# Expert weights loaded with consecutive rows to a partition, and transposes that pick every eighth or second column

## The reference, cut to what matters

```python
def routed_experts(hf, idx, wts, w_gate, w_up, w_down):
    # assignments (token, expert) sorted by expert, padded to blocks of 128 of one expert each
    def one_block(args):
        tok_b, gate_b, e = args
        xb = xpad[tok_b]                                        # (128, 1024)
        hb = jax.nn.silu(xb @ w_gate[e]) * (xb @ w_up[e])       # (1024, 256) each
        return (hb @ w_down[e]) * gate_b[:, None]               # (256, 1024)
    out = lax.map(one_block, ...)
    return jax.ops.segment_sum(out, tok, num_segments=T + 1)[:T]
```

## Time and profile before

| | |
|---|---|
| median of three runs | 3056.81 us |
| the profiled execution's own time | 3048.61 us |
| its span, first to last instruction | 3046.6 us |
| mean granted TensorE clock | 0.926 |
| TensorE busy | 2628.0 us (86%) |
| VectorE busy | 1775.5 us (58%) |
| ScalarE busy | 1059.2 us (35%) |
| GpSimd busy | 937.6 us (31%) |
| moved by the transfers | 519.10 MB, mean 170 GB/s |

### The profile page before, as it was taken

How to read it: one execution, slowest core, us unless ns; L and a number is a source line. 1 busy time by engine, 2 the same in 40 slices (tenths; PEclk the granted TensorE clock), 3 DMA queues, 4 the chain that set the end, 5 groups by cost and what they waited for, 6 DMA issues and landing times.

```text
span 3046.6 us, 55986 instructions
## 1 busy us (share of the span) xinstructions
PE 2628.0 (86%) x11778; PEld 2009.8 (66%) x11779; DVE 1775.5 (58%) x3601; ACT 1059.2 (35%) x2213; POOL 937.6 (31%) x1175
## 2 busy tenths in 40 slices
PE   6898898878887739999999999999998999999930
PEld 1175675566567328877788777877887878878820
DVE  1025886787778653265554566666645554455457
ACT  1022222221211123254444455555544443444411
POOL 0022213423340442323333233333233233333347
PEclk9999898989896759999999999999999999999965
DMA  7961001101101225578886798898977877768665
GB/s 261 333 241 46 31 35 56 42 35 42 42 8 70 87 85 149 110 216 226 236 231 189 213 275 258 250 278 257 275 193 220 248 213 199 193 194 231 153 201 195
DMA packets 255945, 519.10 MB, mean 170 GB/s; under 512 B 18238, under 2 KB 154391, under 8 KB 255732
## 3 DMA queue, kind: packets, MB, share of 16 engines
q1 hardware_dynamic: 199108, 327.34, 31.3%
q0 software_dynamic: 56768, 191.00, 26.3%
HBM read 387.00 MB, written 131.99 MB: 170 GB/s over the span
## 4 chain that ended last, share of the span: by engine, by line
PE 60%; issue 11%; DVE 10%; POOL 8%; ACT 4%; DMA 3%; ACTq 2%; DVEq 1%; SPq 0%; POOLq 0%
PE zb L1483 28%; PE mx L1483 14%; DVE mx L918 4%; PE zb L1317 4%; PE tp L1496 4%; POOL list_d L515 4%; PE mx L1339 3%; PE zb L1281 2%; ACT b_wh L803 2%; DMA b_big<-in_w_ada 2%; PE zb L1432 1%; DVE b_wl L1183 1%; PE ly L1529 1%; POOL b_pa L488 1%; POOL b_fst L477 1%
## 5 line engine op out<-in xcount | busy, mean ns | idle before, releaser
L1483 PE MATMUL zb<-b_wh,b_xh 128*128 (+1 forms) x1456 | 588.6, 404 | 32.7 <-DVE b_wl L1183 29.2
L601 POOL DMA_INDIRECT acc_d<-b_ob,b_sidx x180 | 301.3, 1674 | 998.1 <-DVE b_ob L1208 518.3
L1483 PE MATMUL zb<-b_wh,b_xl 128*128 (+1 forms) x1456 | 575.1, 395 | 0.0
L1483 PE MATMUL zb<-b_wl,b_xh 128*128 (+1 forms) x1456 | 574.1, 394 | 0.0
L1183 DVE TENSOR_TENSOR b_wl<-b_win,b_wh (+1 forms) x780 | 481.0, 685 | 154.7 <-ACT b_wh L803 154.7
L803 ACT CAST b_wh<-b_win (+1 forms) x780 | 419.7, 621 | 150.7 <-issue 86.8
L918 DVE SCALAR_TENSOR_TENSOR mx<-b_a_buf,b_wdw,mx 128x256 f32<-128x256 f32 x928 | 364.2, 481 | 0.0
L1317 PE MATMUL zb<-b_hT,b_win 128*128 128x256 f32 x1536 | 342.9, 386 | 0.8 <-DVE b_mrow L878 0.8
L1483 PEld LDWEIGHTS zb<-b_wh,b_xh 128*128 128x128 f32 x1456 | 277.3, 190 | 88.1 <-issue 35.4
L1160 DVE SCALAR_TENSOR_TENSOR b_hh<-b_sgx,b_lt,zb 128x256 f32<-128x256 f32 x181 | 86.6, 479 | 418.5 <-ACT b_sgx L788 417.5
L1317 PEld LDWEIGHTS zb<-b_hT,b_win 128*128 128x128 f32 x1536 | 296.9, 194 | 46.1 <-ACT b_mixP L666 1.7
(11 more groups left out here) (245 smaller groups left out, 3160.6 us busy)
## 6 DMA issues: line engine op xcount, KB each, us to landing
b_win<-in_w_gate SPq DMA_DIRECT2D x64, 1024.0 KB
b_win<-in_w_up SPq DMA_DIRECT2D x64, 1024.0 KB
b_win<-in_w_down SPq DMA_DIRECT2D x64, 1024.0 KB
b_big<-in_w_ada SPq DMA_DIRECT2D x12, 2048.0 KB, 8.9
acc_d<-b_x1b SPq DMA_DIRECT2D x1, 9216.0 KB, 35.8
b_xin<-in_x_prompt SPq DMA_DIRECT2D x16, 512.0 KB, 3.3
b_big<-in_w_ada_final SPq DMA_DIRECT2D x4, 2048.0 KB, 8.0
b_xres<-in_x_prompt SPq DMA_DIRECT2D x16, 512.0 KB
```

Source lines behind the costliest of these rows:

```text
L601: G.indirect_dma_start(acc_d, bass.IndirectOffsetOnAxis(ap=sidx[i][:, 0:1], axis=0), ob[i][:], None, compute_op=ALU.add).then_inc(S["scatb ...
L1483: last = M.matmul(o, lhs, rhs, start=(first and n == 0), stop=(final and n == len(terms) - 1))
```

## The change

The three weight loads read consecutive rows for a partition: partition p of group k now gets input row 8 p + k of gate and up, and row 2 p + k of down. A partition's rows of one matrix are then 8 KB that lie together in DRAM. On the chip nothing moves: group k still stands in unit k, and each 1 KB row of gate lies beside one of up. To match, the k-th token transpose takes columns k, k + 8, k + 16 and so on, and the k-th hidden transpose columns k, k + 2 and so on. Counts of instructions and transfers, queues and waits stay. The shared expert's weights go through the same function.

```diff
         def load_w(set_, gate, up, down):
-            sp.dma_start(stage_gu[:, set_, 0:UG, 0, :], gate.rearrange("(k p) n -> p k n", p=P)).then_inc(S["w_landed"], 16)
-            sp.dma_start(stage_gu[:, set_, 0:UG, 1, :], up.rearrange("(k p) n -> p k n", p=P)).then_inc(S["w_landed"], 16)
-            sp.dma_start(stage_d[:, set_].rearrange("p (k n) -> p k n", k=KE), down.rearrange("(k p) n -> p k n", p=P)).then_inc(S["w_landed"], 16)
+            sp.dma_start(stage_gu[:, set_, 0:UG, 0, :], gate.rearrange("(p k) n -> p k n", p=P)).then_inc(S["w_landed"], 16)
+            sp.dma_start(stage_gu[:, set_, 0:UG, 1, :], up.rearrange("(p k) n -> p k n", p=P)).then_inc(S["w_landed"], 16)
+            sp.dma_start(stage_d[:, set_].rearrange("p (k n) -> p k n", k=KE), down.rearrange("(p k) n -> p k n", p=P)).then_inc(S["w_landed"], 16)
...
-                    last = M.transpose(tp[h][:, kk * P:(kk + 1) * P], xg[j][:, k * P:(k + 1) * P], ident[:])
+                    last = M.transpose(tp[h][:, kk * P:(kk + 1) * P], xg[j][:].rearrange("t (p k) -> t k p", k=KD)[:, k, :], ident[:])
...
-                last = M.transpose(ly[:, k * P:(k + 1) * P], hh[:, k * P:(k + 1) * P], ident[:])
+                last = M.transpose(ly[:, k * P:(k + 1) * P], hh[:].rearrange("t (p k) -> t k p", k=KE)[:, k, :], ident[:])
```

## The result

The changed kernel takes 3059.14 us (median of 20 runs, 3054.20 to 3066.40); the kernel before takes 3054.85 us beside it (20 runs, 3047.42 to 3060.17). The ratio is 1.0016, with a 95% interval of 1.0009 to 1.0023: some 5 us longer, between 2.7 and 7.0. The ratio lies inside the 0.2% (6 us) that the prediction called no change; the upper end of the interval is just outside it. The prediction said 3168 us, 109 us too much. What happened is its rival (1), the load that stays hidden, whose time was 3057 with 3051 to 3063 around it. That the time lies in the stated range of 3050 to 3215 is owed to the room made for this rival, not to the sum.

The account below looks back on a forecast made before the run. TensorE was taken to bound the expert stage. Slower token-transpose loads added 144 us, stalls gave back 33, transfers and hidden transposes counted nothing: +111 us on 3056.8, so 3168 us, range 3050 to 3215.

Parts of the forecast that it names:

- rival (1): Token transposes: a gap at most doubles the weight load, which stays hidden under the identity pass; 3057 us, chance 0.31.
- the sum: Whole kernel: net +111 us, giving 3160 us for the profiled execution and 3168 us on the median's scale.
- What bounds the kernel: Expert stage: TensorE sets the pace, busy 1723.65 of 1790 us; added TensorE time reaches the end unless a stall swallows it.
- The transfers are worth nothing: Weight loads: they wait for buffers, not buffers for loads, so faster loads gain nothing; bound -22.1 us.
- Rival (3): Weight loads matter after all and the load path hides the gap: up to 22 us faster, around 3040 us; chance 0.06.
- Rival (4): Larger reads push the scatters back until output buffers fill: about 3150 us with a hidden load; chance 0.04.
- The identity pass of 110 ns: Token transposes: streaming the identity, not loading the weights, sets their pace, so each load has 110 ns to hide in.
- the two rows: Transpose load records, 30 columns in 96 ns and 128 in 140: streaming 0.45 ns a column, 57 ns for 128.
- The price of a gap: Token transposes' weight load: 1.74 ns for each separate place, from VectorE's 256-byte-step reduction; 223 ns for 128 columns.
- the term of 144 us: Token transposes: seven loads a block each pay 113 ns, 0.79 us a block, over 182 blocks.
- The hidden transposes take nothing: Two hidden transposes a block: 8 bytes is nearer to the contiguous 4 than to 256, so no cost; upper bound 20 us.
- The cover by stalls: TensorE's idle time ahead of down's first load, 38.9 us in 54 turns, gives back an estimated 33 us.

Follow-up runs that it names:

- the probe: Kernel before plus chains of transposes, matmuls and VectorE additions at several column steps; weight load 62 ns side by side, 110 at step 8, 147 at step 64.
- the kernel whose stalls ahead of down are gone: Kernel before with ScalarE's and VectorE's table reads moved earlier, 3017.89 us; with the change on top 3030.94 us, ratio 0.9927 to the kernel before.

## Why the prediction was wrong

**What bounds the kernel: right.** The stage goes at TensorE's pace: 0.05 us more a block shows at the end as 8.9 us less what stalls swallow, and, within the accuracy of the runs, all of it where there are none.

**The transfers are worth nothing: right, and for the reason given.** The loads alone are at 0.9999, and a load takes as long as before. The reading that the wait named after the transfer was the table reads was confirmed by moving the reads. Rival (3), faster by the loads, needed that wait to be the transfer's. Rival (4), slower by the scatters, did not occur either: the packets of gate and up did not grow, and the loads alone cost nothing. What I had not priced is how little slack a load has, less than 6 us.

**The identity pass of 110 ns sets the pace of the transposes: right.** The probe has 109 ns, and 62 ns for the load beneath it, where the two rows gave 57.

**The price of a gap: the step that failed.** The prediction took 1.74 ns a column from VectorE's reduction and made 223 ns of a load. TensorE's load takes 110 ns at the step of the change, 0.86 ns a column, half the assumed price. It is just the point where the prediction said that the case turns, "110 ns of streaming, 0.86 ns a column". So the term of 144 us was to be about nothing; the 0.88 us for eight transposes and the record of 189 ns come close to the sign that the prediction gave for case (1). The argument for the row was that a float with no neighbour beside it is the same at 32 as at 256 bytes, and that a fetch takes a time whichever engine asks. Both halves fall, though a time it is: at a granted clock of 0.50 and of 1.00 the strided load takes the same 110 ns. On VectorE the gap itself costs 0.65 to 0.88 ns, and the rest of the 1.74 is its own pace of 1.07 ns. On TensorE 256 bytes is an odd distance, 147 ns where 32 bytes takes 110. Had the change stepped by 256 bytes, the seven loads of a block would each have stood out by 147 - 109 = 38 ns, 7 x 38 x 182 = 48 us; this is an estimate from the probe.

Advanced Engine Details and Errata, section "SBUF Cachelines", of the Trainium skill says that it takes at least two hits on a line of 16 bytes to absorb the latency of an access. The probe agrees for the operand that streams (3.7 us side by side, 3.7 for pairs, 3.8 for a step of 2, 7.6 for a step of 8) and for VectorE (359, 358, then 484 and more). It does not agree for the load of weights: a step of 2 has two hits on each line and takes 120 ns against 62. The prediction's reading of it as half the pace, which the section does not state, would have given the better number for the load: 2 x 62 = 124 ns, where 1.74 ns a column gave 223.

**The hidden transposes take nothing: the reason was wrong, the size a few microseconds off.** 8 bytes is not "nearer to the 4": by the probe its load takes 120 ns against 62. The identity pass of 109 ns hides all but 11 of them, by estimate 181 x 2 x 11 = 4 us where the prediction had nothing. The part alone measured 0.05% to 0.23%, some 1.5 to 7 us; the bound from above, 20 us, held.

**The cover by stalls: right in kind.** I expected 33 of 38.9 us of idle time to be used up by 144 us of lateness. The lateness was only 8.9 us, and the idle time ahead of down fell by 6.1 us, to 32.8. In the kernel whose stalls ahead of down are gone there was no such cover, and the change cost some 13 us instead of 5, though the two intervals meet at their ends. One bound of the sum was loosely worked: at 1.6 ns a column with all 38.9 us of cover the low end is 3139, not 3130; nothing hangs on it.

**What stays open.** The step of a block grew by 0.049 us, and the chain spreads it over all four pieces, the matmuls included, whose own operands did not change. The eight token transposes and the two hidden ones account for 0.01 each; of the rest more than half lies in the first ten of gate and up's 24 matmuls, while the later ones follow every 227 ns as before. Why the matmuls behind the transposes are slower too, and why the two kinds of transposes do not add up, was not isolated.

## What to carry to other kernels

A gap between elements is priced for the engine and the operand that reads it: the same step of 8 bytes was free for VectorE and for TensorE's streamed operand and doubled its weight load. Then ask what covers the longer operation, and by how much: here a pass of 109 ns covered a load of 110, a margin of nothing, which a row from another engine could not have decided either way. A small price that stalls hide comes back when the stalls are removed, so measure it again after the next improvement.

## What the runs showed of the hardware

- A load of 128 float32 columns as weights takes 62 ns side by side, 110 to 120 with any gap tried from 8 to 128 bytes and at 384 bytes, 123 at 252 and 260 bytes, and 147 at 256. At half the granted clock the load side by side takes 107 ns, and the strided one (32 or 64 bytes) still 110.
- 8 KB that lie together in DRAM are still moved in packets of 1 KB where they land in rows of 1 KB: 154391 packets under 2 KB in both kernels.
- A read of a table value into a register takes 0.28 us at the median, and in the kernel before up to 1.56 us. At an earlier place in the turn ScalarE's first read is hardly shorter, up to 1.46 us; only its place differs, and with the reads of ScalarE and VectorE moved there the kernel was 1.1% faster. ScalarE's first read of a turn by line (ns min/median/max), in the kernel before and with the reads moved:

```profile
L822 ACTq TENSOR_LOAD <-b_btab x180: 273/282/1562, 1148.7 to 2909.2; - x180
```

```profile
L820 ACTq TENSOR_LOAD <-b_btab x180: 273/282/1462, 1142.4 to 2870.3; - x180
```
